# A hybrid decoder layer on one core: attention starts inside the fourth query projection, half a projection between its steps

## The chip, the cores and the metric

One core of a Trainium2 chip runs one launch of the kernel. The metric is the device time of the launch in microseconds (us), median over runs. Engines: TensorE (PE: matmuls; PEld: its weight loads), VectorE (DVE), ScalarE (ACT), GpSimd (POOL) and the sync engine (SP), which issues most DMAs. Each engine runs its own instructions in order and waits for the others by semaphores.

## What is computed

One layer for 528 prompt tokens (16 learned meta tokens and 512 of the prompt) and 8 decode tokens:

```python
x = x + 0.5 * SwiGLU_1(rmsnorm(x))                    # FFN, 1024 -> 2816 -> 1024
u, q, k, v = split(rmsnorm(x) @ w_in)                 # 512, 8 heads x 64, 2 x 64, 2 x 64
q, k = rope_first_quarter(rmsnorm(q)), rope_first_quarter(rmsnorm(k))
# pooling: 4 channel groups g, trailing mean over w = 2, 4, 8, 16 positions
pool_g = ((mean_w(u_g) - u_g) @ pool_w[g]) * pool_scale_g
# attention: window 128, blocks of 128 queries against 256 keys, a sink in the softmax
p = exp(s - m) / (sum(exp(s - m)) + exp(sink - m));   attn = p @ v
x = x + concat(pool, attn) @ w_out
x = x + 0.5 * SwiGLU_2(rmsnorm(x))
```

The outputs are y of both kinds of token and the new pooling, k and v states.

## The kernel before

Activations lie transposed (channels on the 128 partitions, all 536 tokens in the free dimension). Every large product is in split precision: a weight tile is split by ScalarE into a high part (`whi`, line L1065, `split_next`) and by VectorE into a low part (`wlo`, L1453), and `product` issues three matmuls for each of 8 row blocks k and each half of the tokens (L580). A weight unit has two slots in `whi`/`wlo`, so the high part of unit c waits until unit c-2 is multiplied, and three slots in `raw`, where the sync engine loads it.

The middle of the kernel, between the two FFNs, is one written-out order for each engine. Units 0 to 9 of `w_in` are k, v, q0 to q3, u0 to u3 (`project(m)`); units `U_OUT` onward are the eight of `w_out` (`out_product(d)`). Between them lie:

- For k and each q (x = 0 to 4): VectorE scales it out of PSUM (`take_z`), ScalarE copies and squares it (`spread_z`), DMAs move 8 rows of each head to their rotation partners (`partner`, 4 DMAs each), VectorE multiplies them by the sine (`rotate`), GpSimd multiplies by the cosine and adds (L2025, L2032). `q_sums(j)` sums the squares of q on TensorE, for the norms.
- Attention in 8 steps i of one block of 128 queries and four heads. Per step: TensorE `scores(i)` (mask and q.k, L925, L931); VectorE `maxima(i)` (L1832 to L1839); ScalarE `exps(i)`; VectorE `normalise(i)` (L1845 to L1848); TensorE `turn_probs(i)` transposes the probabilities (L940); ScalarE copies them (`out_probT`, L1349); TensorE `attend(i)` (L949); ScalarE `out_hi(i)`, VectorE `out_lo(i)` (L1855) split the output and free the PSUM banks of the step. Steps use three pairs of banks in turn: scores(i) needs out_lo(i-3) (`olo_ready`).
- Pooling groups: `take_u(g)` on VectorE, `window_sums(g)` on GpSimd (1 to 4 additions of shifted copies, L2013), `pool_mean(g)` on VectorE, `pool_map(g)` on TensorE (L905), `pool_out(g)`, `pool_hi(g)`, and `pool_lo(g)` on GpSimd (L2045).
- The 8 decode tokens: `decode_scores`, `decode_turn`, `decode_turn_back`, `decode_attend` (L961 to L981) and small VectorE work.

The order of TensorE before: q0 to q3, u0, u1 with all sums, `pool_map(0)`, scores 0 and 1, u2 with the decode scores; then the eight steps, in which the only large work is u3 in three pieces (after steps 1, 2, 3) and three blocks of output product 1 (in step 6).

Of the kernel before, what the change touches and what calls it, by code (L numbers as in the profile page):

```python
# [39 lines left out]
P = 128  # L40
# [16 lines left out]
WINDOWS = (2, 4, 8, 16)  # L57
STATE = 15
# [46 lines left out]
PAIR_USES = ["k", "v", "q0", "q1", "q2", "q3", "u0", "u1", "P0", "u2", "P1", "u3", "P2", "so", "P3"]  # L105
PAIR1 = {"v", "q1", "q3", "u1"}


NORM_AT = (1, 2, 5)
SQSUM_AT = (0, KD - 1, 2 * (KD - 1))  # L110
WARM = 4
# [35 lines left out]
def build(nc, a):  # L147
# [44 lines left out]
    hid, _ = place("hid", [P, NT])  # L192
    upn, _ = place("upn", [P, NT])
# [3 lines left out]
    t4, _ = place("t4", [P, KC, NH_ALL])  # L197
# [32 lines left out]
    prob, _ = place("prob", [P, 2, GQ, 2 * P], offset=xhi_end)  # L230
# [23 lines left out]
    dscore, _ = place("dscore", [HD, P], offset=o)  # L254
# [4 lines left out]
    dzsq, o = place("dzsq", [P, NDEC, GQ], offset=o)  # L259
    assert o <= raw_at  # L260
# [10 lines left out]
    banks_of = [ps[:, 2:4, :], ps[:, 4:6, :], ps[:, 6:8, :]]  # L271
    outpair = [ps[:, 0:2, :], ps[:, 6:8, :]]
# [64 lines left out]
    dprobs_kept = sem("dprobs_kept")  # L337
    warmed = sem("warmed")
# [70 lines left out]
    summed_at = {0: 1, 1: 3, 2: 6, 3: 10}  # L409
# [26 lines left out]
    def head_of(i, k):  # L436

        return k // 2, 2 * (i % 2) + k % 2
# [5 lines left out]
    def step_sinks(v, i):  # L444

        return two_by_two(v)[:, :, 2 * (i % 2):2 * (i % 2) + 2]

    def qscale(i, k=None):

        if k is not None:  # L450
            g, j = head_of(i, k)
            c = (j * QT + i // 2) * KVH + g
            return qnrm[:, 1, c:c + 1]
        return qnrm[:, 1, :].rearrange("p (j t g) -> p g j t", j=GQ, t=QT)[:, :, 2 * (i % 2):2 * (i % 2) + 2, i // 2]
# [8 lines left out]
    def _(sp):  # L463
# [49 lines left out]
        for k in ORDER:  # L513
            sp.dma_start(xT[:, k, :], a["x"][:, k, :]).then_inc(x_loaded[k], 16)
            if k == 0:
                sp.dma_start(raw[:, 0, FIRST:KD, :].rearrange("p t c -> p (t c)"), a["gu1"][:, FIRST * P:KD * P]
                             ).then_inc(raw_loaded[0], 16)
# [14 lines left out]
        for m in range(IN_UNITS):  # L532
            load(U_IN + m, a["w_in"], m * KD * P)
        load(U_OUT, a["w_out"], 0)
# [34 lines left out]
    def _(pe):  # L569
        def product(c, dst, tiles, x, n, wait_k=None, ks=None, at=None):  # L570

            if ks is None or ks[0] == 0:
                pe.wait_ge(wlo_ready, c + 1)
            for k in ks or range(tiles):
# [3 lines left out]
                for w, lo in ((whi, 0), (whi, 1), (wlo, 0)):  # L578
                    for h in range(2):
                        last = nc.tensor.matmul(dst[:, h, 0:n], w[:, c % 2, kk, :], x(k, lo, h),  # L580
                                                start=(k == 0 and w is whi and not lo),
                                                stop=(k == tiles - 1 and w is wlo))
            if not ks or ks[-1] == tiles - 1:
# [95 lines left out]
        def plain_products_2():  # L679
# [6 lines left out]
            def plain(j, ks=None, wait_k=None):  # L686
                if ks is None or ks[0] == 0:
                    pe.wait_ge(evacuated, E_A2 + j - 1)
                product(U_A2 + j, pair[j], KD, x_split(n), n, wait_k, ks, chunk)
# [4 lines left out]
            norm_spread(2, META, n, 5)  # L694
# [148 lines left out]
        def q_sums(j):  # L843

            if j == 0:
                pe.wait_ge(tok_ready, 2)
            pe.wait_ge(zg_ready, j + 2)
            for t in range(QT):
                c = (j * QT + t) * KVH
                last = nc.tensor.matmul(nsum[:, 0, c:c + KVH], zsq[:, (j + 1) % 2, META + t * P:META + (t + 1) * P],  # L850
                                 headsel[:, :], start=True, stop=True)
            if j == GQ - 1:
# [5 lines left out]
                last.then_inc(nsum_filled, 1)  # L858
            else:
                last.then_inc(zsq_read, 1)  # L860
# [24 lines left out]
        project(4, half[0])  # L885
        q_sums(0)
        project(4, half[1])
        project(5, half[0])
        q_sums(1)
        project(5, half[1])  # L890
        project(6, half[0])
        q_sums(2)
        project(6, half[1])

# [5 lines left out]
        def pool_map(g):  # L900
# [3 lines left out]
            for s in range(2):  # L904
                last = nc.tensor.matmul(dst[:, s, 0:NH_OUT], poolw[:, g, :], gate[:, s * NH_OUT:(s + 1) * NH_OUT],  # L905
# [3 lines left out]
        def scores(i):  # L909

            t = i // 2
            if i < 2:
                pe.wait_ge(masks_made, 1)
                pe.wait_ge(rot_ready, 5)
                pe.wait_ge(root_ready, 4)
                pe.wait_ge(evacuated, E_USE["u1"] + 1)
            elif i == 2:
                pe.wait_ge(dscores_kept, 2)
            else:
                pe.wait_ge(olo_ready, i - 2)  # L920
            if i == 3:
                pe.wait_ge(dprobs_kept, 1)
            dst = [banks_of[i % 3][:, j // 2, (j % 2) * 2 * P:(j % 2 + 1) * 2 * P] for j in range(GQ)]
# [20 lines left out]
        def attend(i):  # L944
            t = i // 2
# [9 lines left out]
        def decode_scores(bs):  # L955

            if bs[0] == 0:
                pe.wait_ge(newk_placed, 1)
                pe.wait_ge(dq_ready, KVH)
            for b in bs:  # L960
                last = nc.tensor.matmul(turn[:, 0, b * HEADS:(b + 1) * HEADS], ckT[:, b, :], dq[:, b, :, :],  # L961
                                        start=True, stop=True)
            if bs[-1] == NDEC - 1:
                last.then_inc(dscores_filled, 1)

        def decode_turn():
            pe.wait_ge(dscores_kept, 1)
            nc.tensor.transpose(turn[0:HD, 0, 0:P], dscoreT[:, :], ident[:, :]).then_inc(dscores_filled, 1)

        def decode_turn_back():  # L970
            pe.wait_ge(dprob_ready, 1)
            pe.wait_ge(probT_ready, 1)
            nc.tensor.transpose(banks_of[0][:, 1, 0:HD], dprob[:, :], ident[0:HD, 0:HD]).then_inc(dprobs_filled, 1)

        def decode_attend():
            dst = use("so")
            pe.wait_ge(newv_placed, 16 * NDEC)
            by_row = dprobT[:, :].rearrange("p (g b j) -> p g b j", g=KVH, b=NDEC)
            for b in range(NDEC):

                last = nc.tensor.matmul(dst[:, 0, b * HEADS:(b + 1) * HEADS], cv[:, b, :], by_row[:, :, b, :],  # L981
                                        start=True, stop=True)
            last.then_inc(pair_filled, 1)

        project(7, half[0])
        q_sums(3)
        project(7, half[1])
        pool_map(0)
# [1158 lines left out]
```

## Time and profile before

| | |
|---|---|
| time, median of 3 | 894.06 us (893.58 to 895.48) |
| profiled execution, its own time | 894.41 us |
| its span (first to last instruction) | 892.6 us |
| busy share: PE, DVE, ACT, POOL | 99%, 74%, 44%, 4% |

The 1.8 us beside the span lie outside what the trace shows. PE counts as busy whenever a matmul is in flight, whatever its clock: the row PEclk has to be read with it. Times in rows of a timeline are from the start of the span.

### The profile page before, as it was taken

To read this page: it belongs to the slowest core of one execution; us is meant where nothing else is said; L and a number is where in the kernel's file an instruction comes from. 1 tells how busy PE (TensorE), PEld (TensorE's weight loads), DVE (VectorE), ACT (ScalarE), POOL (GpSimd) and SP (SyncE) were. 2 spreads that over 40 slices of the span, in tenths; PEclk is the share of its full clock that TensorE was granted. 3 is DMA by queue.
4 is the path that set the end of the run, shared out by engine and by line. 5 is a ranking of instruction groups with operands and counts; after the bars stand their busy time and mean duration, and the time that the engine had idled before them with its cause. 6 is when DMAs were issued, how large, how long until landed. Compare 5 with 4: busy or idle time off the path is not lost.

```text
span 892.6 us, 17068 instructions
## 1 busy us (share of the span) xinstructions
PE 879.5 (99%) x7100; PEld 861.9 (97%) x7100; DVE 659.2 (74%) x956; ACT 393.6 (44%) x635; POOL 32.4 (4%) x37
## 2 busy tenths in 40 slices
PE   8999999999999999999988999999999999999998
PEld 7999999999999999999867999999999999999998
DVE  7969556997479976743777588997469984699844
ACT  8635213554135544433455446554125552255520
POOL 0000000000000000013322000000000000000000
PEclk9999999999999999999988999999999999999999
DMA  7233313422333323423201323433424424244241
GB/s 260 102 122 127 131 48 123 144 89 94 131 119 119 119 84 119 158 86 100 95 1 45 124 71 118 125 113 101 148 73 153 130 74 153 78 146 131 80 122 61
DMA packets 43180, 98.57 MB, mean 110 GB/s; under 512 B 4288, under 2 KB 5056, under 8 KB 43104
## 3 DMA queue, kind: packets, MB, share of 16 engines
q1 hardware_dynamic: 41056, 94.67, 32.0%
q10 hardware_dynamic: 2048, 2.81, 0.9%
q8 instruction: 56, 0.92, 0.4%
q14 instruction: 20, 0.16, 0.1%
HBM read 93.53 MB, written 3.60 MB: 109 GB/s over the span
## 4 chain that ended last, share of the span: by engine, by line
PE 93%; DVE 4%; ACT 1%; issue 1%; DMA 0%; POOLq 0%; SPq 0%; POOL 0%; DVEq 0%
PE ps L580 44%; PE ps L709 15%; PE ps L711 15%; PE ps L710 15%; PE ps L611 1%; ACT prob L1337 1%; DVE small L1832 1%; DVE prob L1848 1%; PE ps L768 1%; DMA raw<-gu 0%; DVE small L1836 0%; DVE wlo L1453 0%; PE ps L931 0%; PE ps L850 0%; PE ps L949 0%
## 5 line engine op out<-in xcount | busy, mean ns | idle before, releaser
L709 PE MATMUL ps<-xhi,whi 128*128 128x260 f32 (+1 forms) x1092 | 310.2, 284 | 0.1
L711 PE MATMUL ps<-xhi,wlo 128*128 128x260 f32 (+1 forms) x1092 | 310.0, 284 | 0.0
L710 PE MATMUL ps<-xlo,whi 128*128 128x260 f32 (+1 forms) x1092 | 309.6, 283 | 0.0
L709 PEld LDWEIGHTS ps<-xhi,whi 128*128 128x128 f32 x1092 | 205.4, 188 | 0.8 <-issue 0.6
L711 PEld LDWEIGHTS ps<-xhi,wlo 128*128 128x128 f32 x1092 | 205.5, 188 | 0.0
L710 PEld LDWEIGHTS ps<-xlo,whi 128*128 128x128 f32 x1092 | 205.4, 188 | 0.0
L1524 DVE TENSOR_TENSOR wlo<-full,whi 128x1024 fp32r<-128x1024 f32 (+1 forms) x117 | 160.3, 1394 | 0.0
L1065 ACT CAST whi<-raw 128x1024 fp32r<-128x1024 f32 (+1 forms) x75 | 75.3, 1004 | 178.3 <-PE ps L580 171.3
L580 PE MATMUL ps<-hhi,whi 128*128 128x268 f32 (+1 forms) x690 | 140.4, 285 | 0.3
L580 PE MATMUL ps<-hlo,whi 128*128 128x268 f32 (+1 forms) x690 | 140.1, 284 | 0.0
L580 PE MATMUL ps<-hhi,wlo 128*128 128x268 f32 (+1 forms) x690 | 139.7, 284 | 0.0
L580 PEld LDWEIGHTS ps<-hhi,whi 128*128 128x128 f32 x690 | 106.7, 188 | 1.1 <-DVE hlo L1580 1.1
L580 PEld LDWEIGHTS ps<-hhi,wlo 128*128 128x128 f32 x690 | 106.9, 188 | 0.0
L580 PEld LDWEIGHTS ps<-hlo,whi 128*128 128x128 f32 x690 | 106.8, 188 | 0.0
L1453 DVE TENSOR_TENSOR wlo<-raw,whi 128x1024 fp32r<-128x1024 f32 (+1 forms) x75 | 88.8, 1184 | 19.2 <-ACT whi L1065 19.0
L1620 DVE SCALAR_TENSOR_TENSOR gate<-ps,rstd 128x536 f32<-128x536 f32 (+1 forms) x47 | 33.2, 707 | 81.6 <-PE ps L580 81.4
L1125 ACT CAST whi<-full 128x1024 fp32r<-128x1024 f32 x39 | 41.1, 1053 | 106.3 <-issue 89.5
L580 PE MATMUL ps<-xhi,whi 128*128 128x268 f32 (+1 forms) x288 | 61.1, 294 | 0.0
L580 PE MATMUL ps<-xlo,whi 128*128 128x268 f32 (+1 forms) x288 | 59.0, 287 | 0.0
L580 PE MATMUL ps<-xhi,wlo 128*128 128x268 f32 (+1 forms) x288 | 59.0, 286 | 0.0
L1139 ACT CAST whi<-full 128x1536 fp32r<-128x1536 f32 x39 | 57.9, 1484 | 0.0
L1509 DVE TENSOR_TENSOR full<-full 128x1024 f32<-128x1024 f32 x39 | 47.4, 1216 | 0.0
(194 smaller groups left out, 1082.6 us busy)
## 6 DMA issues: line engine op xcount, KB each, us to landing
full<-gu SPq DMA_DIRECT2D x78, 512.0 KB, 4.3
raw<-d SPq DMA_DIRECT2D x32, 448.0 KB, 3.5
full<-gu SPq DMA_DIRECT2D x39, 256.0 KB, 2.7
raw<-d SPq DMA_DIRECT2D x16, 512.0 KB, 3.6
raw<-w_in SPq DMA_DIRECT2D x10, 512.0 KB, 3.7
raw<-gu SPq DMA_DIRECT2D x9, 512.0 KB, 3.6
raw<-w_out SPq DMA_DIRECT2D x8, 512.0 KB, 4.5
xT<-x SPq DMA_DIRECT2D x8, 268.0 KB, 5.6
```

Source lines behind the costliest of these rows:

```text
L580: last = nc.tensor.matmul(dst[:, h, 0:n], w[:, c % 2, kk, :], x(k, lo, h), start=(k == 0 and w is whi and not lo), stop=(k == tiles - 1 an ...
L611: done = nc.tensor.matmul(dst[:, h, 0:n], w[:, c % 2, t, :], x(k, lo, h), start=(first and t == 0 and i == 0), stop=(last and t == KD - 1 ...
L709: nc.tensor.matmul(dst, whi_t, xhi_t, start=(first and pr == 0), stop=False, skip_group_check=True)
L710: nc.tensor.matmul(dst, whi_t, xlo_t, start=False, stop=False, skip_group_check=True)
L711: last = nc.tensor.matmul(dst, wlo_t, xhi_t, start=False, stop=(pr == KC - 1), skip_group_check=True)
L1065: nc.scalar.copy(whi[:, c % 2, 0:t, :], raw[:, c % RAW, 0:t, :]).then_inc(whi_ready, 1)
L1125: nc.scalar.copy(whi7[:, i % 2, 0:2, :], full[:, i % 3, 0:2, :]).then_inc(hi_ready[0], 1)
L1139: nc.scalar.copy(whi7[:, i % 2, 4:7, :], full[:, i % 3, 4:7, :]).then_inc(hi_ready[2], 1)
L1453: nc.vector.tensor_tensor(wlo[:, c % 2, 0:t, :], raw[:, c % RAW, 0:t, :], whi[:, c % 2, 0:t, :].bitcast(F32), ALU.subtract).then_inc(wlo_r ...
L1509: nc.vector.tensor_tensor(full[:, r, 1:5:3, :], full[:, r, 1:5:3, :], full[:, r, 0:7:6, :], ALU.add).then_inc(added, 1)
L1524: nc.vector.tensor_tensor(wlo7[:, i % 3, b, :], full[:, i % 3, b, :], whi7[:, i % 2, b, :].bitcast(F32), ALU.subtract).then_inc(lo_ready[g ...
L1620: nc.vector.scalar_tensor_tensor(out=halves(gate[:, cols], n), in0=pair[d % 2][:, :, 0:n], scalar=-0.5, in1=halves(rstd[:, cols], n), op0= ...
```

## The change

The weights are permuted on the host (`GROUPS = (3, 2, 1, 0)`), so that the pooling group with the widest window (four additions) is projected and worked on first and the narrowest last. The query norm is done for q0 and q1 apart from q2 and q3 (`q_root(0)`, `q_root(1)`; this adds one change to the square root table and back on ScalarE). An attention step now takes heads of one half (q0, q1) for all four blocks first (steps 0 to 3), then of the other (steps 4 to 7). So scores 0 and 1 stand in the middle of q3's projection, and half a projection stands between most steps. The partner DMAs are issued by the sync engine between weight loads, not by ScalarE. Output products 0 and 1 are cut so that their last row block, which needs the last pooling group, comes at the end of each. The prob buffer moves, so GpSimd's additions and splits no longer wait for `prob_ready` or `dprob_ready`. At the start of the kernel the second block of x is loaded and split ahead of the rest of the first weight unit, and six warm-up matmuls stand in place of four.

```diff
-WARM = 4
+WARM = 6
...
-    banks_of = [ps[:, 2:4, :], ps[:, 4:6, :], ps[:, 6:8, :]]
-    outpair = [ps[:, 0:2, :], ps[:, 6:8, :]]
+    banks_of = [nsum, turn, pair[1]]
+    outpair = [pair[1], pair[0]]
...
+        for m in range(4):
+            load_in(m)
+        send_partner(0)
+        load_in(4)
+        load_in(5)
+        for x in range(1, 5):
+            send_partner(x)
+            load_in(x + 5)
         load(U_OUT, a["w_out"], 0)
...
+        scores(0)
+        scores(1)
+        project(5, half[1])
+        project(6, half[0])
+
+        turn_probs(0)
+        scores(2)
+        attend(0)
+        q_sums(2)
+        q_sums(3)
+        project(6, half[1])
+
+        turn_probs(1)
+        scores(3)
+        attend(1)
+        decode_scores()
+        project(7, [0, 1])
         decode_turn()
+        project(7, [2, 3])
+
+        turn_probs(2)
+        scores(4)
+        attend(2)
+        project(7, half[1])
+
+        turn_probs(3)
+        pool_map(0)
+        scores(5)
+        attend(3)
+        decode_turn_back()
+        project(8, half[0])
...
+        turn_probs(7)
+        pool_map(2)
+        attend(7)
+        out_product(0, [3, 2, 4, 5])
+        pool_map(3)
+        out_product(0, [6, 7, 1])
+        out_product(1, [3, 2, 4, 5, 6, 7, 1])
+        out_product(0, [0])
+        out_product(1, [0])
...
-                if (g, s) in after_probs:
-                    pool.wait_ge(prob_ready, after_probs[g, s])
```

Names and lines in the rows below: L608, L971, L956, L962, L980 of the changed kernel are L580, L940, L925, L931, L949 of the one before.

**TensorE around step 1.** Before (`turn_probs(1)`, `scores(3)`, `attend(1)`, then u3; `fixed` holds the identity of the transposes):

```order
L973 MATMUL ps<-fixed,dprob 128x64 [waits probT_ready,dprob_ready]
L905 MATMUL ps<-gate,poolw 128x260 [waits pooled,evacuated]
L905 MATMUL ps<-gate,poolw 128x260
L940 MATMUL ps<-fixed,prob 128x128 [waits prob_ready]
L940 MATMUL ps<-fixed,prob 128x128 x7
L925 MATMUL ps<-maskb,identb 128x512 [waits dprobs_kept,olo_ready]
L925 MATMUL ps<-maskb,identb 128x512
L931 MATMUL ps<-kT,qT 128x256 x4
L949 MATMUL ps<-probT,tok 64x256 [waits probT_ready]
L949 MATMUL ps<-probT,tok 64x256 x3
L580 MATMUL ps<-xhi,whi 128x268 [waits wlo_ready,evacuated]
```

Now (the end of u0's second half, then the same step):

```order
L608 MATMUL ps<-xhi,wlo 128x268 x2
L608 MATMUL ps<-xhi,whi 128x268 x2
L608 MATMUL ps<-xlo,whi 128x268 x2
L608 MATMUL ps<-xhi,wlo 128x268 x2
L971 MATMUL ps<-fixed,prob 128x128 [waits prob_ready]
L971 MATMUL ps<-fixed,prob 128x128 x7
L956 MATMUL ps<-maskb,identb 128x512 [waits root_ready,olo_ready]
L956 MATMUL ps<-maskb,identb 128x512
L962 MATMUL ps<-kT,qT 128x256 x4
L980 MATMUL ps<-probT,tok 64x256 [waits probT_ready]
L980 MATMUL ps<-probT,tok 64x256 x3
```

Ahead of the step there stood one small product; now half a projection does, and the decode scores follow.

**TensorE at the end of output product 1.** Before (its last row blocks, and the first row of output product 2, which waits for `wlo_ready`):

```order
L580 MATMUL ps<-mhi,wlo 128x260 x2
L580 MATMUL ps<-mhi,whi 128x260 x2
L580 MATMUL ps<-mlo,whi 128x260 x2
L580 MATMUL ps<-mhi,wlo 128x260 x2
L580 MATMUL ps<-mhi,whi 128x260 [waits wlo_ready,evacuated]
```

Now (the end of product 1 without its last block, that of product 0, that of product 1, then product 2):

```order
L608 MATMUL ps<-mhi,whi 128x260 x2
L608 MATMUL ps<-mlo,whi 128x260 x2
L608 MATMUL ps<-mhi,wlo 128x260 x2
L608 MATMUL ps<-mhi,whi 128x260 x2
L608 MATMUL ps<-mlo,whi 128x260 x2
L608 MATMUL ps<-mhi,wlo 128x260 x2
L608 MATMUL ps<-mhi,whi 128x260 x2
L608 MATMUL ps<-mlo,whi 128x260 x2
L608 MATMUL ps<-mhi,wlo 128x260 x2
L608 MATMUL ps<-mhi,whi 128x260 [waits wlo_ready,evacuated]
L608 MATMUL ps<-mhi,whi 128x260
```

Product 0 used to end five blocks ahead of product 2; now it ends one block ahead of it.

**VectorE ahead of the first pooling product**, now (`maxima(4)`, `out_lo(2)`, three of decode, `pool_mean(0)`, `take_u(1)`); before, `pool_mean(0)` and `take_u(1)` stood ahead of all steps:

```order
L1904 SCALAR_TENSOR_TENSOR small<-small,nsink 128x4 [waits step]
L1907 TENSOR_TENSOR small<-small,fixed 128x4 [waits step]
L1923 TENSOR_TENSOR mlo<-ps,mhi 128x2x128 [waits ohi_ready]
L2001 TENSOR_TENSOR dsmall<-dsmall 64x1 [waits dexp_ready]
L2002 RECIPROCAL dsmall<-dsmall 64x1 [waits step]
L2003 TENSOR_SCALAR dprob<-dprob,dsmall 64x128 [waits step]
L1872 SCALAR_TENSOR_TENSOR gate<-wsum,up 128x512 [waits summed,zg_ready]
L1874 COPY ulast<-up 128x15
L1875 COPY stT<-up 128x8
L1876 TENSOR_REDUCE dsum<-stT 128x8 [waits step]
L1877 SCALAR_TENSOR_TENSOR gate<-dsum,up 128x8 [waits step]
L1836 TENSOR_TENSOR up<-ps,rstd 128x536 [waits unit_done]
```

All of this now lies in the stretch in which TensorE runs attend 2, half of u1 and `turn_probs(3)`.

## Rows read from the trace of the kernel before

**Rows 1.** Page: span, and the TensorE clock granted in 40 slices (tenths).
```profile
span 892.6 us, 17068 instructions
...
PEclk9999999999999999999988999999999999999999
```

**Rows 2.** Who TensorE waited for: us in total, times, longest us.
```profile
PE ps L949 <- ACT probT L1349: 3.3, 4, 1.8
PE ps L925 <- DVE mlo L1855: 2.4, 2, 1.9
```

**Rows 3.** Windows: length, then PE, PEld, DVE, ACT, POOL busy, PEclk, DMA share, GB/s.
```profile
451.00:458.00 7.00, 5.92 (x27) 3.96 (x26) 4.66 (x16) 4.90 (x15) 1.28 (x1) 0.51 0.00 0
...
482.00:489.00 7.00, 6.91 (x32) 6.40 (x31) 5.90 (x18) 3.29 (x10) 1.30 (x1) 0.52 0.20 50
```

**Rows 4.** Timeline, TensorE, steps 0 and 1: start, us, what [idle before <-releaser].
```profile
442.68 1.04 PE L940 MATMUL ps<-fixed,prob 128*128 128x128 f32 x8
443.56 0.59 PE L925 MATMUL ps<-maskb,identb 128*128 128x512 bf16 x2
...
446.16 0.27 PE L973 MATMUL ps<-fixed,dprob 64*128 64x64 f32 x1
...
447.35 1.04 PE L940 MATMUL ps<-fixed,prob 128*128 128x128 f32 x8
450.27 0.60 PE L925 MATMUL ps<-maskb,identb 128*128 128x512 bf16 x2 [1.89 <-DVE mlo L1855]
```

**Rows 5.** Timeline, TensorE: u3 blocks, decode_attend, last ten output blocks, output product 2.
```profile
467.80 0.52 PE L580 MATMUL ps<-xhi,whi 128*128 128x268 f32 x2
...
470.14 1.04 PE L940 MATMUL ps<-fixed,prob 128*128 128x128 f32 x8
...
480.66 2.50 PE L981 MATMUL ps<-dprobT,cv 128*128 128x8 f32 x16
...
495.74 0.51 PE L580 MATMUL ps<-mhi,whi 128*128 128x260 f32 x2
...
503.02 0.40 PE L580 MATMUL ps<-mhi,whi 128*128 128x260 f32 x2
```

**Rows 6.** Timeline, VectorE, after the first output product.
```profile
499.63 0.70 DVE L1967 TENSOR_TENSOR xT<-ps,xT 128x520 f32<-128x520 f32 x1 [5.40 <-PE ps L580]
500.77 1.23 DVE L1453 TENSOR_TENSOR wlo<-raw,whi 128x1024 fp32r<-128x1024 f32 x1 [0.44 <-ACT whi L1065]
```

**Rows 7.** Timeline, VectorE: maxima twice, pooling mean, normalise, maxima.
```profile
434.29 1.21 DVE L1832 TENSOR_REDUCE small<-ps 128x4 f32<-128x1024 f32 x1
...
436.01 1.21 DVE L1832 TENSOR_REDUCE small<-ps 128x4 f32<-128x1024 f32 x1
...
450.80 0.68 DVE L1804 SCALAR_TENSOR_TENSOR gate<-wsum,up 128x512 f32<-128x512 f32 x1
...
452.20 0.16 DVE L1845 TENSOR_TENSOR small<-small 128x4 f32<-128x4 f32 x1
...
453.67 1.22 DVE L1832 TENSOR_REDUCE small<-ps 128x4 f32<-128x1024 f32 x1
```

**Rows 8.** One line on VectorE: times, duration ns min/median/max, first and last start.
```profile
L1836 DVE SCALAR_TENSOR_TENSOR small<-small,nsink x8: 161/163/1177, 435.7 to 482.1; 128x4 f32<-128x4 f32 x8
...
L1453 DVE TENSOR_TENSOR wlo<-raw,whi x75: 1084/1215/1932, 13.6 to 880.5; 128x1024 fp32r<-128x1024 f32 x43, 128x896 fp32r<-128x896 f32 x32
```

**Rows 9.** Timeline: k rotation sent and taken; q1 split, its rotation sent.
```profile
386.93 3.23 ACTq L1328 DMA_DIRECT2D partner<-zg  x4
...
393.13 0.71 DVE L1785 TENSOR_TENSOR sq<-partner,sinT 128x536 f32<-128x536 f32 x1
...
403.46 1.05 ACT L1065 CAST whi<-raw 128x1024 fp32r<-128x1024 f32 x1 [4.12 <-PE ps L580]
...
405.80 2.64 ACTq L1328 DMA_DIRECT2D partner<-zg  x4
```

**Rows 10.** Timeline, TensorE, at the start of the kernel.
```profile
7.66 0.82 PE L611 MATMUL ps<-xhi,whi 128*128 128x268 f32 x2 [1.58 <-ACT xhi L1075]
```

More of the change, by code:

```diff
@@ L953, in attend, with decode_scores @@
                         last.then_inc(attended, 1)
[L955 to L961, printed above, removed]
+        def decode_scores():
+            pe.wait_ge(newk_placed, 1)
+            pe.wait_ge(dq_ready, KVH)
+            pe.wait_ge(probT_ready, 2)
+            for b in range(NDEC):
+                last = nc.tensor.matmul(turn[:, 1, b * HEADS:(b + 1) * HEADS], ckT[:, b, :], dq[:, b, :, :],
@@ L988, in _, with out_product, mixed_there @@
-        pool_map(0)
+            last.then_inc(douts_filled, 1)
+        def out_product(d, ks=None):
+            begin, end = (NG - 1, 0) if d < 2 else (0, KD - 1)
+            if ks is None or ks[0] == begin:
+                if d == 0:
+                    pe.wait_ge(olo_ready, 6)
+                elif d == 1:
+                    pe.wait_ge(evacuated, E_OUT)
+                else:
+                    pe.wait_ge(evacuated, E_OUT + d - 1)
+            def mixed_there(k):
+                if d < 2 and k < NG:
+                    pe.wait_ge(plo_ready, GROUPS.index(k) + 1)
+                elif d < 2 and k < NG + 2:
+                    pe.wait_ge(dolo_ready, 1)
+                elif d < 2:
+                    pe.wait_ge(olo_ready, 2 * QT)
+            product(U_OUT + d, outpair[d % 2], KD, columns(mhi, mlo, 0, NH_OUT), NH_OUT, mixed_there, ks,
+                    begin=begin, end=end)
@@ new lines, in _ @@
+        project(7, [2, 3])
[9 more added lines that the diff above has]
+        project(8, half[0])
+        turn_probs(4)
+        scores(6)
+        attend(4)
+        decode_attend()
+        project(8, half[1])
+        turn_probs(5)
+        pool_map(1)
+        scores(7)
+        attend(5)
+        project(9, half[0])
+        turn_probs(6)
@@ L1921, in _ @@
         nc.vector.tensor_tensor(dsmall[:, 2:3], dsmall[:, 1:2], dsink, ALU.add).then_inc(dnmax_ready, 1)
-        pool_mean(1)
+        normalise(3)
+        maxima(4)
+        out_lo(2)
         dve.wait_ge(dexp_ready, 1)
@@ new lines, in _ @@
+        dve.wait_ge(zg_ready, 5)
+        pool_mean(0)
+        take_u(1)
+        normalise(4)
+        pool_out(0)
+        maxima(5)
+        out_lo(3)
+        dve.wait_ge(dprobs_filled, 1)
+        nc.vector.tensor_copy(dprobT[:, :], nsum[:, 1, 0:HD]).then_inc(dprobs_kept, 1)
+        split_next(7)
+        normalise(5)
+        maxima(6)
+        out_lo(4)
+        dve.wait_ge(douts_filled, 1)
+        for g in range(KVH):
+            rows = slice(g * HD, (g + 1) * HD)
+            last = nc.vector.tensor_copy(dout[rows, :, :],
+                                         turn[rows, 1, 0:HD].rearrange("p (b h) -> p b h", b=NDEC)[
+                                             :, :, g * GQ:(g + 1) * GQ])
@@ L1963, in _ @@
+        last.then_inc(douts_kept, 1)
+        pool_mean(1)
+        take_u(2)
+        normalise(6)
+        pool_out(1)
+        maxima(7)
+        split_next(8)
+        out_lo(5)
+        normalise(7)
+        pool_mean(2)
+        out_lo(6)
+        take_u(3)
+        pool_out(2)
+        split_next(9)
+        out_lo(7)
+        pool_mean(3)
+        pool_out(3)
         for d in range(KD):
```

382 lines of the change are left out of this document (164 added, 218 removed).

## The prediction

> **What bounds the kernel now.** I read the page first: the span is 892.6 us, TensorE is busy for 99% of it, and the granted clock is at nine tenths or more everywhere but in the 21st and 22nd slice, 446 to 491 us [rows 1]. So nothing but TensorE's time counts, and the only stretch in which much of it is lost is the attention. The list of TensorE's waits names what is lost there as idle time: 3.3 us for `probT` and 2.4 us for `mlo`, 5.7 us together [rows 2]. The windows show a second loss. From 451 to 458 and from 482 to 489 the mean clock is 0.51 and 0.52, that is, mostly the lower level of 1.2 GHz where 2.4 GHz is the upper; with 5.92 and 6.91 us busy, that is 5.92 x 0.49 = 2.9 and 6.91 x 0.48 = 3.3 us of lost work [rows 3]. The first of them follows directly on the 1.89 us wait in front of `scores(3)` [rows 4]: there `turn_probs(1)` is done, the banks of step 0 have to be freed by VectorE, and between `attend(0)` and `scores(3)` TensorE had nothing but one small product and a transpose, 1.19 us plus 0.9.
>
> To get the whole loss I compare a sum with the clock on the wall. From `turn_probs(0)` at 442.68 to output product 2 at 503.02 lie 60.3 us [rows 4, 5]. The work in it at full clock: 8 turns at 0.88 (442.68 to 443.56) = 7.0; six scores with their attends at 2.60 (443.56 to 446.16) = 15.6, and two attends more at about 1.0 = 2.0; three pooling products and a decode transpose, 1.19 for one with the transpose, 3.2; u3 at 2.34 per three blocks = 6.2; the decode values, 2.5 us with a part at the lower clock, taken as 1.9; 16 output blocks at (503.02 - 495.74) / 10 = 0.73, 11.6. The sum is 47.5, the loss 12.8. Idle time and clock explain 5.7 + 6.2 = 11.9 of it; the other 0.9 are slow first matmuls behind the gaps.
>
> **The change part by part.** No matmul is removed or added but two warm-up ones: the same products stand in another order. Ahead of 442.68 TensorE shows no wait, so the new order has 12.8 us to win in this stretch and no more.
>
> *Half a projection between steps.* Four blocks are 4 x 0.78 = 3.1 us [rows 5]. `scores(i+2)` needs the banks of step i-1: after `attend(i-1)` come a copy on ScalarE and a small one on VectorE, and 3.1 us and a turn now cover them. `turn_probs(i)` needs maxima (1.72 us), four exponentials on ScalarE and normalise (1.47 us) after its scores [rows 7]; two half projections and a step lie between them, over 9 us. So both waits in [rows 2] go, and with them what let the clock fall: minus 12.8 us. What is late next I looked for by walking through the four in-order queues with the durations above. Most waits have one to five us to spare; these four do not.
>
> (a) `attend(0)` needs the copy of `probT`, which on ScalarE now stands behind both first exponentials and the spread of q3. I find it ready 0.5 us before TensorE, if VectorE is not held up on the way. One hold-up of VectorE by GpSimd costs it (1177 - 163) ns = 1.0 us in the small operations and (1932 - 1215) ns = 0.7 us in the weight split [rows 8]. With one there, 0.4 us of wait; bounds 0 and 1.4.
>
> (b) `pool_map(0)` needs `pool_mean(0)` and `take_u(1)`, which used to lie ahead of the steps. From the end of `scores(4)` TensorE has an attend, half of u1 and a turn, 1.0 + 3.1 + 0.9 = 5.0 us. VectorE has maxima 1.72, about 1.0 for `out_lo(2)` and the three decode operations, the mean 1.40, then the take, 0.7 (as the similar operation in [rows 6]): 4.8 us, 0.2 to spare. In the 5 us ahead GpSimd adds four times for this group, with no wait for `prob_ready` any more. Each addition can hold VectorE for up to 1.0 us [rows 8], and VectorE has some 2 us of idle time there: between 0 and 2.0 us of wait; I take 1.0, half of it. The Trainium skill speaks against this edit: "SBUF — State Buffer", section Who interferes with whom, says that a VectorE instruction with two SBUF inputs and a GpSimd one that reads SBUF exclude each other, the later one standing for the whole of the earlier. By it all four additions are paid in full and the wait is the upper bound; the trace shows such hold-ups in single operations and far fewer than GpSimd has instructions, so I stay with the half.
>
> (c) `pool_map(3)` has only four output blocks, 2.9 us, as cover after `attend(7)`. VectorE has to do a weight split, an `out_lo` and the mean, 1.2 + 0.4 + 1.4 = 3.0 us after a take that it can do early. Wait 0 to 1.5, taken as 0.7.
>
> (d) Output product 2 needs the low part of its weights. Its slot is free only when product 0 is done. Before, VectorE starts on product 0's result at 499.63 and finishes that weight split at 500.77 + 1.23 = 502.0, so it takes 2.4 us from the end of product 0, and 3.6 us of product 1 cover it [rows 5, 6]. Now product 0's last block stands one block ahead of product 2. The cover is 0.73 us: a new wait of 1.65 us, surely.
>
> *The rotations sent by SP.* Four DMAs take 2.6 to 3.2 us of the issuing queue and landed at most 393.13 - 390.16 = 3.0 us after [rows 9]; ScalarE is freed from that, which costs nothing and gains nothing there, since it was idle. What waits is `scores(0)`: after q1 is projected, 2.3 us of split and spread (403.46 to 405.80), 2.6 of issue, at most 3.0 of landing, 0.7 on VectorE, 1.3 on GpSimd, 9.9 us, against q2, two sums of 0.8 and half of q3, 5.8 + 1.6 + 2.9 = 10.3. So it is hidden, with 0.4 us or more to spare. On SP each send stands between weight loads that are needed several us later.
>
> *Square root table twice more.* Two table loads at a place where ScalarE waits for TensorE anyway; 0 us, and at most what (a) shows where that slack is gone.
>
> *The start.* The second matmul group waits 1.58 us for `xhi` [rows 10], with the cast of the other weights ahead of it on ScalarE. The swap takes that cast behind it, but the pass ends with the last of eight x blocks on the same engine, which only gains what ScalarE idled: bounds 0 and 1.1, taken as 0.4. Two more warm-ups lie in front of data that isn't there yet.
>
> Later loads of w_out wait for the last `pool_mean`, which now comes after the steps, but some 9 us of products 0 and 1 and then all of product 2 follow it; hidden.
>
> **Sum.** 894.41 (the profiled execution: 892.6 and 1.8 outside) - 12.8 - 0.4 + 0.4 + 1.0 + 0.7 + 1.65 = 885.0. It ran 0.35 above the median, so against the median of 894.06 I predict 884.6.
>
> **The rivals.**
> 1. The clock falls again. For: (b) and (d) are waits of a size near the 1.89 us behind which it fell. Against: they stand between dense projections, where the one before stood among transposes and other waits. A fall costs about 3.1 us [rows 3]: 887.7 with one, 890.8 with two. Chance 0.20.
> 2. The order is cleaner than I think, only (d) is left, and the start gives 1.1: 894.06 - 12.8 - 1.1 + 1.65 = 881.8. Chance 0.10.
> 3. The rotations come late, because on SP's queue they stand behind 512 KB loads. Then `rotate(2)` and `rotate(3)` hold VectorE, which runs in order, and with it the first maxima. Landing one load later, some 3.5 us, takes 3.1 us at `scores(0)` and perhaps 2 at `scores(2)`: 890. The load in front is issued some 4 us earlier and should have landed. The Trainium skill, "DMA: Bandwidth & Descriptors", Queues, rings and completion order, has each ring consume descriptors in order, which is what this rival needs; no row here shows it. Chance 0.06.
> 4. Slower. VectorE becomes the bound: in steps 3 to 7 it has maxima 1.7, normalise 1.5, and a mean, a take, a pooling output or a weight split, some 6.5 us per step of 6.7 on TensorE. If GpSimd's 14 operations each hold it for 1.0 us, it is 14 us behind, less some 6 of slack: 8 us of waits in four places, each with a fall of 3.1. 884.6 + 8 - 2 + 12 = 903. It decides once the new waits and falls pass 13 us. The hold-ups were only some six before, so 0.04.
>
> **How the numbers follow.** My forecast has 0.60, from 882.5 to 887. The range for 8 in 10 takes in rival 2 and one to two falls: 881.5 to 890. A measurement of this kernel tells about 0.2% (1.8 us) from no change. Faster by more: everything but rival 4 and the worst of rivals 1 and 3, 0.92; within 0.2%: 0.03; slower: 0.05.
>
> **What the profile afterwards would show.** TensorE's waits for `mlo` at scores gone, those for `probT` below 1 us; one wait of 1.5 to 1.8 us for `wlo` at output product 2, whose start lies some 11 us ahead of 503.02 less what the start gave; `pool_map(0)` waiting for VectorE up to 2 us; the clock row without its dips. I am wrong if `scores(0)` waits for `rot_ready`, if the clock still falls in the stretch, or if VectorE's operations beside GpSimd's additions are stretched in most steps.

## The result and the profile after

The changed kernel takes 889.57 us in the median of seven runs (887.77 to 890.92), the one before 893.58 us beside it; the ratio is 0.995, 95% interval 0.9939 to 0.996. Faster, as forecast, but by 4 us where 9.5 were forecast: 889.57 lies inside the range of 881.5 to 890 and 5 us above the number. The profiled execution took 889.57 us, with a span of 887.8.

The page and the list of TensorE's waits after, which answer to [rows 1, 2]:

```profile
span 887.8 us, 17081 instructions
...
PEclk9999999999999999999999999999999999999999
```

```profile
PE ps L608 <- DVE wlo L1520: 1.8, 1, 1.8
PE ps L630 <- DVE hid L1509: 1.2, 1, 1.2
PE ps L998 <- DVE dscoreT L1980: 1.2, 1, 1.2
...
PE ps L980 <- ACT probT L1390: 0.8, 2, 0.6
PE ps L608 <- DVE act_gate L1886: 0.7, 1, 0.7
PE ps L930 <- DVE gate L1877: 0.6, 1, 0.6
```

The wait for `mlo` is gone, that for `probT` fell from 3.3 us to 0.8, and the dip in the clock row is gone. In the attention and output part TensorE now has six waits, 5.18 us together: 1.84 at output product 2 (L608 for `wlo`), 1.17 at `decode_turn` (L998), 0.24 at `attend(4)` and 0.60 at `attend(6)` (L980), 0.71 at the first half of u2's projection (L608 for `act_gate`: it needs a bank that `pool_out(0)` frees), and 0.62 at `pool_map(3)` (L930). Behind the longest of them the clock falls. TensorE's timeline, and the windows there (length, then PE, PEld, DVE, ACT, POOL busy, PEclk, DMA share, GB/s):

```profile
439.22 0.30 PE L998 MATMUL ps<-fixed,dscoreT 128*64 128x128 f32 x1 [1.17 <-DVE dscoreT L1980]
...
452.95 0.51 PE L608 MATMUL ps<-xhi,whi 128*128 128x268 f32 x2 [0.71 <-DVE act_gate L1886]
...
496.60 0.48 PE L608 MATMUL ps<-mhi,whi 128*128 128x260 f32 x2 [1.84 <-DVE wlo L1520]
```

```profile
498.00:500.00 2.00, 2.00 (x12) 2.00 (x11) 2.00 (x3) 1.03 (x2) 0.00 (x0) 0.50 1.07 401
500.00:502.00 2.00, 2.00 (x13) 2.00 (x13) 1.92 (x5) 0.01 (x1) 0.00 (x0) 0.66 0.90 328
```

That is 2 x 0.50 + 2 x 0.34 = 1.7 us of lost work at the level of 1.2 GHz; from 502 on the mean is 1.00 again.

On VectorE, `normalise` scales the probabilities by four operations. The same line in the kernel before, and after:

```profile
L1848 DVE TENSOR_SCALAR prob<-prob,small x32: 340/348/1381, 439.0 to 487.8; 128x256 f32<-128x256 f32 x32
```

```profile
L1916 DVE TENSOR_SCALAR prob<-prob,small x32: 340/348/1466, 420.0 to 475.7; 128x256 f32<-128x256 f32 x32
```

Minimum, median and maximum are nearly alike; the difference is how often the long ones come. The timelines show it: the four take 1.14 us in a step left alone, and in steps 2, 4 and 6 of the changed kernel

```profile
432.35 4.72 DVE L1916 TENSOR_SCALAR prob<-prob,small 128x256 f32<-128x256 f32 x4
...
448.64 3.59 DVE L1916 TENSOR_SCALAR prob<-prob,small 128x256 f32<-128x256 f32 x4
...
465.99 2.65 DVE L1916 TENSOR_SCALAR prob<-prob,small 128x256 f32<-128x256 f32 x4
```

while GpSimd's window sums run in the same microseconds:

```profile
432.18 1.07 POOL L2091 TENSOR_TENSOR wsum<-up 128x528 f32<-128x528 f32 x1 [1.08 <-DVE up L1836]
433.32 3.60 POOL L2091 TENSOR_TENSOR wsum<-wsum 128x528 f32<-128x528 f32 x3
...
448.46 1.07 POOL L2091 TENSOR_TENSOR wsum<-up 128x528 f32<-128x528 f32 x1 [11.54 <-DVE up L1836]
449.60 2.21 POOL L2091 TENSOR_TENSOR wsum<-wsum 128x528 f32<-128x528 f32 x2
```

Four additions, four scalings, 4.7 us for both: each scaling stands for one whole addition. With three additions, 3.6 us. In the kernel before, one step of eight was stretched (2.17 us, beside one of GpSimd's splits).

### The profile page after: what moved, and what is told of

Read it like the earlier page. It is cut to its first block, busy times and chain, and to the rows that moved or that the text cites. A ratio compares the mean times of both kernels' runs of the same rounds, so it can differ in the third digit from the quotient of the medians.

```text
span 887.8 us, 17081 instructions
## 1 busy us (share of the span) xinstructions
PE 876.8 (99%) x7104; PEld 859.7 (97%) x7104; DVE 663.6 (75%) x957; ACT 397.0 (45%) x639; POOL 32.6 (4%) x37
## 4 chain that ended last, share of the span: by engine, by line
PE 93%; DVE 4%; ACT 1%; issue 1%; DMA 1%; SPq 0%; DVEq 0%; ACTq 0%
PE ps L608 43%; PE ps L737 15%; PE ps L739 15%; PE ps L738 15%; PE ps L639 1%; DVE prob L1916 1%; PE ps L796 1%; DMA raw<-gu 1%; DVE wlo L1520 1%; PE ps L962 0%; PE ps L980 0%; ACT prob L1381 0%; PE ps L880 0%; DVE small L1900 0%; PE ps L654 0%
## 5 line engine op out<-in xcount | busy, mean ns | idle before, releaser
L608 PE MATMUL ps<-hhi,whi 128*128 128x268 f32 (+1 forms) x690 | 140.4, 285 | 0.3
L608 PE MATMUL ps<-hlo,whi 128*128 128x268 f32 (+1 forms) x690 | 140.1, 284 | 0.0
L608 PE MATMUL ps<-hhi,wlo 128*128 128x268 f32 (+1 forms) x690 | 139.7, 284 | 0.0
L608 PEld LDWEIGHTS ps<-hhi,whi 128*128 128x128 f32 x690 | 106.8, 188 | 1.1 <-DVE hlo L1647 1.1
L608 PEld LDWEIGHTS ps<-hhi,wlo 128*128 128x128 f32 x690 | 107.0, 188 | 0.0
L608 PEld LDWEIGHTS ps<-hlo,whi 128*128 128x128 f32 x690 | 106.8, 188 | 0.0
L608 PE MATMUL ps<-xhi,whi 128*128 128x268 f32 (+1 forms) x288 | 60.5, 291 | 0.7 <-DVE act_gate L1886 0.7
L608 PE MATMUL ps<-xhi,wlo 128*128 128x268 f32 (+1 forms) x288 | 58.7, 285 | 0.0
L608 PE MATMUL ps<-xlo,whi 128*128 128x268 f32 (+1 forms) x288 | 58.5, 285 | 0.0
```

## The experiments

Twelve kernels, each compared with the kernel before on the same chip. Where one is set against the changed kernel, it is by the two ratios to before, if nothing else is said.

**Output product 0 finished earlier**

```diff
-        out_product(1, [3, 2, 4, 5, 6, 7, 1])
+        out_product(1, [3, 2])
         out_product(0, [0])
-        out_product(1, [0])
+        out_product(1, [4, 5, 6, 7, 1, 0])
```

> The last block of output product 0 is put ahead of blocks 4, 5, 6, 7, 1 of output product 1, instead of behind them; nothing else of the changed kernel is touched. Theory: output product 2 waits 1.84 us at 496.60 for the low half of its weights, because that half can be taken only when product 0 is complete, and the granted clock falls behind that wait (0.50 for some 2 us). Finishing product 0 five blocks (some 3.3 us) earlier removes the wait, and with it the fall (1.6 us): about 3.4 us below the changed kernel, ratio to before about 0.991, TensorE's wait at output product 2 at 0, PEclk about 1.0 in 496 to 501. Rival A: the clock falls on its own there, as it did elsewhere in the kernel before; then only the wait goes, 1.8 us. Rival B: the attention and pooling blocks that product 0 now needs earlier are not there (pool_map(3)'s gate waits 0.62 us already) and the wait moves ahead of product 0's last block: 0 to 1 us gained.

Measured: 887.28 us, ratio 0.992 (0.9908 to 0.9933), 2.7 us below the changed kernel. The wait at product 2 is gone and the clock is at 1.00 from 490 to 520; the others stand:

```profile
PE ps L998 <- DVE dscoreT L1980: 1.2, 1, 1.2
PE ps L980 <- ACT probT L1390: 0.8, 2, 0.6
PE ps L608 <- DVE act_gate L1886: 0.7, 1, 0.7
PE ps L930 <- DVE gate L1877: 0.6, 1, 0.6
```

Rival B is out. Between the theory and rival A the time does not decide, since 2.7 lies between 3.4 and 1.8. The mean clock speaks for rival A: it is 1.000 in one of this kernel's five runs and in three of the changed kernel's seven, so in these few runs falls as such became no rarer. Its trace has a fall of the clock elsewhere, with TensorE busy all through and no wait ahead of it:

```profile
429.00:430.00 1.00, 1.00 (x7) 1.00 (x6) 0.10 (x1) 0.98 (x3) 1.00 (x1) 0.50 0.02 8
430.00:431.00 1.00, 1.00 (x6) 1.00 (x6) 0.00 (x0) 0.83 (x3) 0.73 (x3) 0.50 0.91 94
```

Over all profiles: six kernels have this wait of 1.8 us, and behind it the clock fell in three (the changed kernel, the held sums, the narrow group first) and stayed at 1.00 in three; in the four where it is removed it never fell there. Whether that is cause or chance six and four profiles can't settle; the wait itself is removed for certain.

**GpSimd's window sums held until the step's probabilities are normalised**

```diff
             src, steps = up[:, g % 2, :], GROUPS[g]
+            if g < 3:
+                pool.wait_ge(prob_ready, (3, 5, 7)[g])
```

> GpSimd's window sums of the first, second and third pooling group start only after the probabilities of step 2, 4 and 6 are normalised; nothing else of the changed kernel is touched. Theory: VectorE's four scalings of a normalise (1.14 us together when alone, 4.72, 3.59 and 2.65 us beside GpSimd's additions) are held up by GpSimd's additions one for one, and the waits of TensorE of 1.17 us (decode_turn), 0.71 us (projection 8) and 0.24 and 0.60 us (attend 4 and 6) are what reaches the path: gated, the four scalings take 1.1 to 1.3 us in each step, these waits shrink to under 0.5 us together, and the time falls by about 2.2 us, ratio to before about 0.9925. Rival A: VectorE's order is too full in any case, the stretched scalings have slack ahead of them, and the waits stay: under 0.5 us. Rival B: the later sums make pool_mean and so pool_map late, a new wait of 1 to 2 us at pool_map(0) or pool_map(1), and the time is that of the changed kernel or above.

Measured: 886.66 us, ratio 0.9916 (0.9904 to 0.9929), 3.0 us below the changed kernel. The scalings, and the waits of TensorE from 395 us on:

```profile
L1916 DVE TENSOR_SCALAR prob<-prob,small x32: 345/349/355, 419.6 to 473.1; 128x256 f32<-128x256 f32 x32
```

```profile
PE ps L608 <- DVE wlo L1520: 1.8, 1, 1.8
PE ps L930 <- DVE gate L1877: 0.6, 1, 0.6
PE ps L980 <- ACT probT L1390: 0.3, 1, 0.3
```

`decode_turn` and u2's first half no longer wait, 0.84 us for `probT` became 0.3: 2.4 of 2.7 us gone, and both rivals with them. The 0.3 us is at `attend(4)`, so the 0.24 us there in the changed kernel is not the additions' doing; the other three, 2.5 us, are. The additions haven't become harmless, they hit other operations now, behind which TensorE shows no wait beyond that 0.3 us:

```profile
436.09 0.98 DVE L1902 TENSOR_TENSOR small<-small,qnrm 128x4 f32<-128x4 f32 x1
...
438.35 2.34 DVE L1520 TENSOR_TENSOR wlo<-raw,whi 128x1024 fp32r<-128x1024 f32 x1
```

**Both**

> Both edits: product 0's last block early, and GpSimd's window sums held until the probabilities of steps 2, 4 and 6 are normalised. Theory: the two act in different places and add up, 3.4 + 2.2 = 5.6 us below the changed kernel, about 884, ratio to before about 0.989, which is where the forecast stood. Rival: the tail's wait comes from VectorE's lateness that the additions cause, so that both edits buy the same time: about the better of the two alone, 886.

Measured: 884.11 us, ratio 0.9887 (0.9871 to 0.9903), 5.6 us below the changed kernel. The two edits add up; the rival is out. From 395 us on TensorE waits 0.6 us at `pool_map(3)` and 0.3 at one `attend`, no more.

**No half projection between steps 0 and 1**

```diff
         q_sums(3)
-        project(6, half[1])
 
         turn_probs(1)
         scores(3)
         attend(1)
+        project(6, half[1])
         decode_scores()
```

> The half of projection 6 between steps 0 and 1 is put behind attend(1), so that steps 0 and 1 stand one behind the other with no half projection between; nothing else of the changed kernel is touched. Theory: the half projections are what hides VectorE's maximum and ScalarE's exponential of the next step; without it TensorE waits 2 to 4 us at turn_probs(1) or scores(3), and the granted clock falls for some 2 us behind it: 3 to 5 us above the changed kernel, ratio to before 0.998 to 1.001. Rival: the two leading steps have enough slack from the two score products at the start, and the time is within 1 us of the changed kernel.

Measured: 898.66 us, ratio 1.0054 (1.0039 to 1.0069), 9 us above the changed kernel: the theory's direction, and twice its size. A wait at `scores(3)` is there, as expected, and behind it a second one at `decode_turn`:

```profile
431.50 0.94 PE L956 MATMUL ps<-maskb,identb 128*128 128x512 bf16 x2 [2.12 <-ACT dnrm L1431]
...
446.91 0.42 PE L998 MATMUL ps<-fixed,dscoreT 128*64 128x128 f32 x1 [4.74 <-DVE dscoreT L1980]
```

```profile
430.00:440.00 10.00, 8.51 (x54) 6.29 (x55) 0.95 (x3) 3.23 (x6) 1.31 (x4) 0.83 0.52 171
440.00:450.00 10.00, 5.26 (x32) 5.05 (x32) 9.66 (x24) 3.99 (x12) 4.37 (x4) 0.76 0.09 17
450.00:460.00 10.00, 10.00 (x67) 7.57 (x65) 6.84 (x22) 5.80 (x16) 1.39 (x2) 0.90 0.09 37
```

2.12 + 4.74 - 1.17 = 5.7 us more idle time, and a clock of 0.83, 0.76 and 0.90 over thirty microseconds, (8.51 x 0.17 + 5.26 x 0.24 + 10 x 0.10) = 3.7 us; against it, the fall behind output product 2 (1.7 us) is missing in this trace. One misplaced half projection costs more than the whole change brings. Not all of it is missing cover, though. `scores(3)` waits for ScalarE's root (`dnrm`), which stands behind the exponentials of step 2. And VectorE, in its fixed order, stands at `take_u(0)` until the late half projection is done; only then come the scalings of step 2, beside GpSimd's four additions:

```profile
440.05 4.71 DVE L1916 TENSOR_SCALAR prob<-prob,small 128x256 f32<-128x256 f32 x4
```

Alone they take 1.14 us, so up to 3.6 of the 4.74 us at `decode_turn` are the hold-up by the additions. No run has this order with the additions held.

**The second sums of the queries split**

```diff
         q_sums(2)
+        project(6, [4])
         q_sums(3)
-        project(6, half[1])
+        project(6, [5, 6, 7])
```

> The kernel with both edits (product 0's last block early, window sums held), and in it block 4 of projection 6 put between the two sums of squares of the query heads, q_sums(2) and q_sums(3), which stood one behind the other (twenty matmuls of 2 columns and 1, some 2.2 us). Theory: the granted clock of 0.50 from 428.4 to 431.5 us in the traces of the three last kernels, without any wait of TensorE ahead of it, comes from this stretch of tiny matmuls; split by 268-column matmuls the fall is gone in this place, and the time is that of the parent's executions at a mean clock of 1.000, some 1 us below its median, about 883.0, minus nothing, plus 0.1 to 0.2 us for one more switch; scores(3), which needs the second sums, still has about 1 us to spare. Rival: the fall comes in this place whatever stands there, and nothing changes (884), or goes to another place.

Measured, on top of both edits: 885.09 us, ratio 0.9899 (0.9884 to 0.9914), not below the parent. The fall came again, behind the second sums: it begins at 429.4 us where the parent's begins at 428.7, and this execution was 0.8 us later already at TensorE's transposes of v (399.63 for 398.82). So splitting the stretch of tiny matmuls by one block neither removed the fall nor moved it, and the theory fails; what brings the fall is open.

```profile
430.00:431.00 1.00, 1.00 (x7) 1.00 (x6) 0.00 (x0) 0.99 (x2) 0.94 (x2) 0.50 0.68 66
```

**The narrowest pooling group first**

```diff
-GROUPS = (3, 2, 1, 0)
+GROUPS = (0, 1, 2, 3)
...
-        out_product(0, [3, 2, 4, 5])
+        out_product(0, [0, 1, 4, 5])
         pool_map(3)
-        out_product(0, [6, 7, 1])
+        out_product(0, [6, 7, 2])
```

> The changed kernel with its pooling groups in the old order, narrowest window first and widest last, the columns of the input weights, the maps and the blocks of the output products with them. Theory: the widest group's four additions of GpSimd (4.7 us) and its mean then stand in front of pool_map(3), where TensorE already waits 0.62 us, in place of the narrowest's one addition (1.1 us): 3 to 4 us of new wait there, given back in part since one addition instead of four stands beside the scalings of step 2 (decode_turn's 1.17 us goes): 2 us above the changed kernel, ratio to before about 0.997. Rival: the order of the groups does nothing, because the blocks of output product 0 ahead of pool_map(3) cover the longer sum: within 0.5 us, or below by the 1.2 us of decode_turn.

Measured: 892.68 us, ratio 0.9985 (0.9974 to 0.9996), 3.1 us above the changed kernel, where the theory had 2. Both halves of it show: `pool_map(3)` waits 3.2 us, `decode_turn` no more. Behind the 3.2 us the clock falls too (0.61, 0.50, 0.50 and 0.69 in the four microseconds from 486), which the theory did not have.

```profile
PE ps L930 <- DVE gate L1877: 3.2, 1, 3.2
```

**The rotations sent by ScalarE in the new order**

```diff
-            sp.wait_ge(zg_ready, x + 1)
...
-                    sp.dma_start(partner[to:to + half, x % 2, c0:c0 + 2 * n],
+            act.wait_ge(zg_ready, x + 1)
...
+                    act.dma_start(partner[to:to + half, x % 2, c0:c0 + 2 * n],
```

> The changed kernel with the copies of the rotated halves sent by ScalarE again, as before, instead of by the sync engine's queue. Forecast's theory: the sends were hidden on ScalarE (0 us gained by the move), and are hidden here: within 0.5 us of the changed kernel. Rival: on ScalarE four sends of 0.66 us per head pair stand ahead of exponentials of steps 0 and 1 that now come beside them, and delay turn_probs by up to 2.6 us: 1 to 3 us above the changed kernel, with a wait at turn_probs(0) or attend(0).

Measured: 896.56 us, ratio 1.0023 (1.0013 to 1.0034), 6.5 us above the changed kernel. The forecast's theory fails and the rival is too small. ScalarE's timeline, and TensorE's step 0:

```profile
423.19 0.57 ACT L1371 ACTIVATE prob<-ps,small,qnrm 128x256 f32<-128x256 f32 x1
...
425.22 2.62 ACTq L1362 DMA_DIRECT2D partner<-zg  x4
427.88 1.01 ACT L1380 COPY probT<-ps 128x1024 f32<-128x1024 f32 x1 [2.69 <-issue]
```

```profile
424.66 1.13 PE L945 MATMUL ps<-kT,qT 64*128 64x256 f32 x8
428.95 1.97 PE L963 MATMUL ps<-probT,tok 128*64 128x256 f32 x8 [3.15 <-ACT probT L1380]
...
430.85 3.36 PE L863 MATMUL ps<-headsel,zsq 128*128 128x2 f32 x15
```

The copy of step 0's probabilities stands behind four sends; TensorE waits 3.15 us, and the mean clock from 430 to 440 is 0.55, another 4.5 us. The fall behind output product 2 (1.7 us) is missing here.

**The rotations sent by the sync engine in the old order** (the same code, in the kernel before)

> The kernel before, with only the rotated halves sent by the sync engine's queue between the loads of the mixer's weights, as in the changed kernel; order of the steps, groups, gates and start are those of before. Forecast's theory: four sends of 0.66 us per pair lie behind nothing that ScalarE owes in that order, since there the steps begin only after the last pair is sent: no difference, within 0.2% of before. With the run that sent them by ScalarE in the new order (7 us slower than the changed kernel) it would say that the move is worth nothing alone and 7 us under the early steps. Rival: the sends cost ScalarE something in the old order too: 1 to 3 us below before.

Measured: 894.39 us, ratio 1.0004 (0.9992 to 1.0016): nothing, as expected.

**The kernel before without its own holds on GpSimd**

```diff
-        after_probs = {(2, 0): 2, (3, 0): 6, (3, 2): 7}
+        after_probs = {}
...
-        pool.wait_ge(dprob_ready, 1)
         pool_lo(0)
...
-        pool.wait_ge(prob_ready, 3)
         pool_lo(1)
```

> The kernel before, without its own four places where GpSimd waits for the probabilities of a step before it adds or splits; nothing else is touched. Theory: those waits kept GpSimd's additions away from VectorE's scalings; without them the scalings of two or three steps stretch by 1 to 3.5 us each as in the changed kernel, in a stretch where TensorE waits for VectorE and ScalarE anyway: 2 to 4 us above the kernel before, ratio 1.002 to 1.005. Rival: GpSimd's sums and splits come earlier, which is worth as much as the stretching costs (pool_map's waits of 1.89 us at 450.27 and 0.5 us at 476.13 shrink): within 0.2% of before, or below.

Measured: 899.34 us, ratio 1.006 (1.0042 to 1.0077), 5.3 us slower, a little above the theory's range. In its profile, 6.1 us longer in span, 2.0 us lie at the start already (ScalarE reaches the first head pair at 387.65 in place of 385.61 us), so the holds are worth 3 to 5 us in this order. Four steps are stretched in place of one, beside additions and splits:

```profile
448.26 3.53 DVE L1848 TENSOR_SCALAR prob<-prob,small 128x256 f32<-128x256 f32 x4
456.39 2.17 DVE L1848 TENSOR_SCALAR prob<-prob,small 128x256 f32<-128x256 f32 x4
...
476.31 1.81 DVE L1848 TENSOR_SCALAR prob<-prob,small 128x256 f32<-128x256 f32 x4
482.72 4.10 DVE L1848 TENSOR_SCALAR prob<-prob,small 128x256 f32<-128x256 f32 x4
```

TensorE pays for it mostly in clock. It has one new wait, at `turn_probs(1)`, but all its waits from 395 to 520 us together grow by 0.9 us only; the work lost at the lower level, by single microseconds (busy time x (1 - clock)), goes from 6.2 to 9.4 us, since both falls last longer:

```profile
PE ps L940 <- DVE prob L1848: 2.3, 1, 2.3
```

**The start undone, and the start alone** (`WARM`, and the block of x behind which the rest of the first weights follows; in the changed kernel back to the old one, in the kernel before the new one)

> The changed kernel with its start as before: four warming matmuls instead of six, and the second piece of the first weights sent behind the first block of x instead of behind the second. The forecast's theory: the start's change is worth 0.4 us (0.31 in the profile after), so this is 0.3 to 0.4 us above the changed kernel, within what the measurement can tell. Rival: the start is worth nothing and its 0.31 us was scatter: no difference, and a wait of 1.6 us at the first low half of x as before that ends at the same time as after.

Measured: 891.11 us, ratio 0.9978 (0.9966 to 0.9991), 1.5 us above the changed kernel in the medians and 2.5 by the ratios.

> The kernel before with the change's start alone: six warming matmuls for four, and the second piece of the first weights sent, rounded and subtracted behind the second block of x. Theory from the profiles so far (ScalarE reaches the first head pair's gain at 385.0 to 386.1 us in the nine with the new start, mean 385.55, and at 385.6 to 387.7 in the four with the old one, mean 386.46): the new start is worth about 0.9 us on average, 893.0 where before is 893.9, ratio about 0.999. Rival, the forecast's term: 0.4 us, and what lies above it in those four profiles is scatter: no difference that the measurement can tell. Both lie near its limit; 1.5 us, the distance of the changed kernel with the old start, would be a third answer.

Measured: 893.23 us, ratio 0.9991 (0.9981 to 1.0001). Between the forecast's 0.4 and the 2.5 above, near 0.9, and within reach of nothing. The profiles say what the start does. With four warm matmuls, those of the first products take mostly 0.65 us per pair, up to 10.2 us in the kernel before and 12.3 us in the changed kernel with its old start; with six they take 0.40 to 0.52 from 6.7 us on in the changed kernel. Here one of each near 9 us, four warm matmuls first:

```profile
8.75 0.65 PE L639 MATMUL ps<-xhi,whi 128*128 128x268 f32 x2
```

```profile
9.36 0.49 PE L639 MATMUL ps<-xhi,whi 128*128 128x268 f32 x2
```

**Both edits, and the last mean ahead of two low halves on VectorE**

```diff
         pool_out(2)
+        pool_mean(3)
         split_next(9)
         out_lo(7)
-        pool_mean(3)
         pool_out(3)
```

> The kernel with both edits (product 0's last block early, window sums held) and a third one on VectorE: the mean of the narrowest pooling group is formed ahead of the weights' low half (1.22 us) and of the low half of the last step's output (0.42 us), behind which it stood. Theory: TensorE's wait of 0.60 us at 483.34 for this mean (1.66 us, beside GpSimd's split of the group before) goes, and the mean, started 1.6 us earlier, also clears that split: 0.6 us below the kernel with both edits, about 883.5, ratio to before about 0.988. Rival: what it passed is late in its turn (output product 0 needs both low halves within 5 us) and the wait moves by the same amount: no change.

Measured: 882.54 us, ratio 0.9881 (0.9863 to 0.9898), below the kernel before by 11.4 us in the medians and 10.6 by the ratio, and the fastest of all. What is left from 395 us on is one wait of 0.3 us, and no stretch of its trace from 400 to 510 us is below a clock of 1.00:

```profile
PE ps L980 <- ACT probT L1390: 0.3, 1, 0.3
```

The wait at `pool_map(3)` went, as the theory has it. Against the parent with both edits it is 1.6 us in the medians and 0.5 by the ratios, but the two intervals overlap, so the size of this step is not measured.

## Why the prediction fell short

The main mechanism was right: the order removes most of the stretch's loss. What the new order brings in its place was not. Put together from the two traces, the profiled time is 894.41 - 11.3 (loss won) - 0.3 (start) + 5.2 (new waits) + 1.6 (clock) = 889.6, where the forecast had - 12.8 - 0.4 + 3.75 + 0 = 885.0. The 11.3 is (503.02 - 399.64) - (496.60 - 399.33 - 5.18), from TensorE's transposes of v to output product 2, and the 0.3 is 399.64 - 399.33; the 1.6 is what lies behind output product 2, 391.2 us after against 389.6 before. So the 4.6 us came in three parts of much the same size: 1.4, 1.6 and 1.5, and 0.1 at the start.

**New waits, 5.2 for 3.75.** This is the step whose mechanism failed, and it is term (b). It counted the first pooling group's four additions only, took them at half a hold-up and let the wait fall on `pool_map(0)`, because "the trace shows such hold-ups in single operations and far fewer than GpSimd has instructions"; the additions of the later groups had no term. The hold-ups were few because the kernel before held GpSimd back: without its holds four of eight steps are stretched in place of one, and it is 5.3 us slower. The change dropped them, and nine of the ten additions met scalings, in steps 2, 4 and 6: four scalings took 4.72, 3.59 and 2.65 us instead of 1.14. They surfaced at other consumers: 1.17 us at `decode_turn` behind the first group's four, for which (b) had 1.0 with a bound of 2.0, and 1.31 us at u2's first half and `attend(6)` behind the five of the next two groups. (a) and (b) themselves, 1.4 us in the sum, are 0. With the additions held back, these 2.5 us are gone and the time is 3.0 us lower. The description of the change ties the dropped holds to the moved `prob` buffer; the kernel before runs without them too, so they were a matter of order there, not of need.

The Trainium skill's "SBUF — State Buffer", section Who interferes with whom, which the forecast set aside, was right about VectorE: it names `tensor_scalar` among the operations that can take the port pair shared with GpSimd, the other engine then standing for the whole instruction. The rows agree, 4.72 us for four scalings beside four additions of 1.07 + 3.60 us, for which it takes 1.14 alone. The wait that the forecast drew from it, the upper bound of 2.0 us at `pool_map(0)`, did not come: that wait is 0.

**The clock, 1.6 for 0.** The sum had no term for it. This is rival 1, at half the price it had: one fall behind (d), 1.6 to 1.7 us where I had taken 3.1 from [rows 3], since those seven microseconds each held a longer one. Its argument, that a wait between dense projections brings none, did not hold here nor in two other kernels, and held in three.

**The gain, 11.3 for 12.8.** The loss was sized nearly right: in the fastest kernel, which has only 0.3 us of waiting left, it is 12.0 us (from the transposes of v to the end 880.3 - 399.02 = 481.3 us against 892.6 - 399.64 = 493.0, and the 0.3). The other 0.7 I put down to slow first matmuls behind the new waits, which [rows 4, 5] had shown behind the old gaps, 0.9 us of them, and of which I counted none; no run separates it. What the last 0.8 is was not taken apart either.

**What held.** (d) is 1.84 for 1.65 us, and gone with product 0 finished earlier; (c) is 0.62 for 0.7. `scores(0)` waits for nothing: the rotations are hidden on the sync engine's queue, so rival 3 is out. Their price of nothing was read against ScalarE's idle time in the old order, where it is true (894.39); in the new order ScalarE isn't idle there, and leaving the sends on it would have cost 6.5 us. The widest group first is worth 3.1 us, for which I had no term. Rival 4 did not come: VectorE's lateness cost TensorE 2.5 us, not 8, and three of eight steps were stretched, not most. The start, 0.4 in the forecast, is 0.8 us alone by the ratio, and 1.5 to 2.5 where it is taken out of the changed kernel: probably larger than I had it, its size not settled: alone it is not told from nothing.

## What to carry to other kernels

When a change drops a wait that no data needs, ask what it kept apart: find the busiest operations of the two engines and lay them beside each other in time. Rows of the old kernel show a hazard at the rate at which the old order let it happen; for a new order, count each instruction that it lays beside the other engine's, at the full hold-up, and follow the queue to the first consumer that has no slack. Here the forecast looked at one consumer and one group of additions; the cost fell on others. And when work moves earlier, what used to be free on an engine, like four DMA sends, has to be priced against what that engine will do then.

## What I had not expected

- The clock falls without any wait. Between 427.9 and 433 us TensorE is busy without a gap and the clock all the same at 0.50 for some 3 us in five of the profiles (product 0 early, the held sums, both, the split sums, the start undone), and not in that of the changed kernel. It costs 1.7 us each time, by windows of single microseconds, and begins 29.0 to 29.9 us behind the transposes of v in all five; what decides it is open.
- A wait of 1.84 us was followed by a fall in three profiles of six, and three of the changed kernel's seven runs had a mean clock of 1.000, with spans of 886.0 to 886.6 us against 887.5 to 888.9 for the others. So executions of one program lie some 2 us apart, and whether the clock fell goes with it.
- The start scatters more than its change is worth: ScalarE reaches the first head pair between 385.0 and 386.1 us in ten profiles with six warm matmuls, and between 385.6 and 387.7 in four with four.
